# Four sequences side by side in the sample attention of a hybrid layer: one change, read from the trace

## What is computed

```python
def sample_layer(x, cache_cmp, cache_slc, cache_win, cache_mem, ...):
    ...
    o_cmp, o_slc = nsa_global(q, pos, full_c, full_s, p, rel_bias)
    o_win = win_attention(q[:, None], pos[None, :], win_kv[:, None], kpos, rel_bias)[:, 0]
    o_nsa = nsa_combine(gn, o_cmp, o_slc, o_win)
    o_mem = mem_attention(qm, cache_mem)

def masked_softmax(s, mask, axes=-1):
    ...
    m = jnp.max(s, axis=axes, keepdims=True)
    e = jnp.where(mask, jnp.exp(s - m), 0.0)
    return e / jnp.maximum(jnp.sum(e, axis=axes, keepdims=True), 1e-30)
```

## Time and profile before

| | us |
|---|---|
| median of the runs | 2143.67 |
| the profiled execution | 2147.72 |
| its span, first to last instruction | 2145.8 |
| the phase of the sample attention in it (328.26 to 526.37) | 198.11 |
| of it round 0, from the first scores of C to the last transposes | 341.7 to 433.5 |
| round 1 | 433.5 to 526.4 |

### The profile page before, as it was taken

How to read it: one execution, slowest core, us unless ns; L and a number is a source line. 1 busy time by engine, 2 the same in 40 slices (tenths; PEclk the granted TensorE clock), 3 DMA queues, 4 the chain that set the end, 5 groups by cost and what they waited for, 6 DMA issues and landing times.

```text
span 2145.8 us, 42699 instructions
## 1 busy us (share of the span) xinstructions
PE 1979.5 (92%) x17225; PEld 1038.0 (48%) x17225; DVE 516.7 (24%) x1342; ACT 407.5 (19%) x960; POOL 335.2 (16%) x359
## 2 busy tenths in 40 slices
PE   7997887788888999995999999999999999999995
PEld 3446773535447888644334444343443434444342
DVE  2224454241650111115211212112121211212111
ACT  3133561011650000000111111111111111111110
POOL 0010000000760000320112121121211112121121
PEclk9997987887999999996899999999999999999997
DMA  8116414231205110001999999999999999999994
GB/s 299 63 49 246 156 51 196 98 138 49 92 1 207 50 59 30 15 30 39 413 390 396 395 395 396 390 397 394 395 396 395 392 391 394 398 394 397 391 398 143
DMA packets 104369, 532.05 MB, mean 248 GB/s; under 512 B 15480, under 2 KB 32640, under 8 KB 52577
## 3 DMA queue, kind: packets, MB, share of 16 engines
q1 hardware_dynamic: 83721, 469.42, 55.4%
q0 software_dynamic: 19824, 59.12, 9.6%
q10 hardware_dynamic: 768, 2.75, 0.3%
HBM read 508.82 MB, written 28.91 MB: 251 GB/s over the span
## 4 chain that ended last, share of the span: by engine, by line
PE 49%; DMA 2%; ACT 1%; issue 0%; DVE 0%; POOL 0%; POOLq 0%; DVEq 0%
PE psum L2425 29%; PE psum L2438 16%; PE psum L2411 1%; PE psum L2474 1%; PE psum L2419 1%; DMA arena<-scr_h,arena 1%; PE psum L2464 1%; DMA y_sum<-arena 1%; ACT arena L2349 1%; POOL y_sum L2320 0%; ACT arena L2354 0%; DVE arena L2376 0%; PE psum L2455 0%; DVE arena L2372 0%; ACT arena L2335 0%
## 5 line engine op out<-in xcount | busy, mean ns | idle before, releaser
L2425 PE MATMUL psum<-arena 128*32 128x512 f32 x6144 | 666.9, 591 | 0.0
L2425 PEld LDWEIGHTS psum<-arena 128*32 128x32 f32 x6144 | 200.9, 108 | 447.3 <-issue 441.5
L2438 PE MATMUL psum<-arena 128*32 128x256 f32 x6144 | 344.8, 379 | 8.2 <-ACT arena L2349 8.2
L2438 PEld LDWEIGHTS psum<-arena 128*32 128x32 f32 x6144 | 191.3, 109 | 143.8 <-ACT arena L2349 15.7
L2390 DVE TENSOR_SCALAR arena<-psum 128x256 f32<-128x256 f32 x96 | 40.8, 425 | 883.0 <-PE psum L2425 880.3
L2320 POOL DMA_INDIRECT y_sum<-arena x96 | 149.3, 1555 | 620.1 <-ACT arena L2354 614.1
L2114 PE MATMUL psum<-arena 128*128 128x272 f32 x768 | 181.8, 394 | 1.4 <-PEq L217 1.4
L2114 PEld LDWEIGHTS psum<-arena 128*128 128x128 f32 x768 | 146.2, 191 | 34.8 <-issue 3.1
L2346 ACT ACTIVATE arena<-arena 128x256 f32<-128x256 f32 x96 | 40.1, 418 | 607.2 <-DVE arena L2390 607.2
L738 PE MATMUL psum<-arena 128*128 128x512 f32 (+3 forms) x320 | 112.5, 510 | 0.2 <-DVE arena L610 0.2
L2354 ACT ACTIVATE arena<-psum,arena 128x256 f32<-128x256 f32 x96 | 45.2, 471 | 187.4 <-PE psum L2438 187.4
(11 more groups left out here) (353 smaller groups left out, 1755.2 us busy)
## 6 DMA issues: line engine op xcount, KB each, us to landing
arena<-in_w_gu SPq DMA_DIRECT2D x256, 1024.0 KB, 20.1
arena<-in_w_down SPq DMA_DIRECT2D x128, 1024.0 KB, 16.9
arena<-in_w_gb SPq DMA_DIRECT2D x24, 512.0 KB, 3.5
arena<-in_w_tok SPq DMA_DIRECT2D x3, 2048.0 KB, 10.3
arena<-in_x_all SPq DMA_DIRECT2D x8, 512.0 KB, 5.9
arena<-in_cache_mem SPq DMA_DIRECT2D x8, 512.0 KB, 3.6
arena<-in_cache_win SPq DMA_DIRECT2D x8, 512.0 KB, 4.1
arena<-in_w_up SPq DMA_DIRECT2D x1, 4096.0 KB, 13.4
```

Source lines behind the costliest of these rows:

```text
L2425: mm = pe.matmul(gu_bank(g)[32 * j:32 * j + 32].rearrange("p (h n) -> p h n", h=2), xgT[:, k, 32 * g:32 * g + 32], w_in_e[:, k, :, 256 * j ...
L2438: mm = pe.matmul(dn_half(g)[32 * j:32 * j + 32], actT[:, g, k % 2, 32 * (k // 2):32 * (k // 2) + 32], w_down_e[:, k, 256 * j:256 * j + 256 ...
```

## The change

Each engine's part of the phase is written anew. A batch is now one branch (for S one chunk) of all four sequences: TensorE turns the keys of all four into four banks (`turn_keys`, 16 transposes) and then issues the four products one behind the other, each in its own 32-column part (`score`). The values follow the same way, chunk outside, sequence inside, with the 32-row product at the end. Bias and maximum are one VectorE instruction on each bank (`biased`, in the profile CUSTOM_DVE with a read of the accumulator), and the maximum over the parts is taken over a few columns. The mask of S is added to the bias on GpSimd. Both rounds of C stand at the front. The order of the other branches is M, S, W in round 0 and M, W, S in round 1. All four memory loads of round 1 wait for all window products of round 0, all four window loads of round 1 for all memory products of round 1, and the gathers of round 1 for all S products of round 0; the third and fourth of these gathers wait also for the memory loads. ScalarE copies the S bias, one bank at a time, in place of VectorE. Buffers that were shared by both rounds are doubled where both are alive.

```diff
+        BATCH = [(0, M, 0)] + [(0, S, q) for q in range(4)] + [(0, W_, 0), (1, M, 0), (1, W_, 0)] + [(1, S, q) for q in range(4)]
...
+                filled(sp, 2, "mv", 0)
+                for s in range(4):
+                    load_window(0, s)
+                filled(sp, 2, "wv", 0)
+                for s in range(4):
+                    load_memory(sp, 1, s)
+                filled(sp, 3, "mv", 1)
+                for s in range(4):
+                    load_window(1, s)
...
                 for r in range(2):
+                    if r:
+                        filled(pool, 3, "sv", 0)
                     for s in range(4):
-                        if r:
-                            pool.wait_ge(s_vu, s + 1)
                         if r and s == 2:
                             pool.wait_ge(s_ml[3], 32)
...
+                    pool.wait_ge(d_pk, r + 1)
+                    pool.tensor_tensor(blocks_of(scores[:, 0:PAST]), blocks_of(bias_slc),
+                                       pick[:, r, 3, 0:32].unsqueeze(1).unsqueeze(3).to_broadcast([128, SUB, 32, 4]),
+                                       ALU.add).then_inc(d_sb, 1)
...
+                def biased(out, scores_in, bias, r, at):
+                    return dve.tensor_tensor_reduce(out, scores_in, bias, -1.0, 3e38, ALU.add, ALU.min, stats[:, r, at:at + 1])
...
+                def quarter(n):
+                    r, _, q = BATCH[n]
+                    filled(dve, n % 2, "S", n)
+                    sl = scores[:, 512 * q:512 * q + 512]
+                    if q == 0:
+                        dve.wait_ge(d_sb, r + 1)
+                    biased(sl, bank(n % 2), sl, r, 6 + q).then_inc(free[n % 2], 1)
...
-                    link(dve.tensor_tensor(blocks_of(scores[:, 0:PAST]), blocks_of(bias_slc),
-                                           pick[:, 3, 0:32].unsqueeze(1).unsqueeze(3).to_broadcast([128, SUB, 32, 4]),
-                                           ALU.add))
-                    keys(r, S)
-
-                    for q in range(4):
-                        dve.wait_ge(s_sp, SP0 * r + 5 + 12 + q + 1)
-                        sl = scores[:, 512 * q:512 * q + 512]
-                        link(dve.tensor_tensor(sl, bank(q), sl, ALU.add))
-                    dve.wait_ge(s_sp, SP0 * r + 22)
-                    link(dve.tensor_tensor(scores[:, PAST:], bank(4)[:, 256:288], bias_new[:, r], ALU.add))
-                    maximum(k + 2, scores)
...
+                def turn_keys(n):
+                    r, kind, q = BATCH[n]
+                    for s in range(4):
...
+                        to_fill(pe, 4 + s, "K", n)
+                        for a in range(4):
...
+                            mm = pe.transpose(bank(4 + s)[:, 128 * a:128 * a + 128], src, ident)
+                        mm.then_inc(full[4 + s], 1)
...
+                        for s, rows in enumerate(rows_of_seq):
+                            mm = pe.matmul(bank(b)[rows], q_rows[:, 4 * r + s], kT(n, s), start=True, stop=True,
+                                           tile_position=(0, 32 * s))
+                    mm.then_inc(full[b], 1)
...
+                    for a in range(SUB + 1):
...
+                        for s, rows in enumerate(rows_of_seq):
+                            lhs, v = (probT[:, a, rows], cache[:, s, 256 * a + 128:256 * a + 256]) if a < SUB else \
+                                     (probT[0:32, 16, rows], v_slc[0:32, 4])
+                            mm = pe.matmul(bank(3)[rows, 0:128], lhs, v, start=(a == 0), stop=(a == SUB),
+                                           tile_position=(0, 32 * s))
```

More of the change, by code:

```diff
@@ new lines, in build_program, with to_fill, filled, emptied @@
+        use_no = {}
+        for b, name in IN_BANKS:
+            use_no[b, name] = sum(1 for b_, n_ in use_no if b_ == b)
+        bank_of = lambda *name: next(b for b, n_ in use_no if n_ == name)
+        def to_fill(pe, b, *name):
+            if use_no[b, name]:
+                pe.wait_ge(free[b], use_no[b, name])
+        def filled(eng, b, *name):
+            eng.wait_ge(full[b], use_no[b, name] + 1)
+        def emptied(eng, b, *name):
+            eng.wait_ge(free[b], use_no[b, name] + 1)
@@ new lines, in _, with exponentials, compressed @@
+                for b in range(4):
+                    filled(act, b, "bias", b)
+                    copy(bias_slc[:, 512 * b:512 * b + 512], bank(b)).then_inc(free[b], 1)
+                def exponentials(kind, r, out, in_, at_max, at_sum, scale=-1.0):
+                    return act.activation(out, in_, ACT.Exp, bias=stats[:, r, at_max:at_max + 1], scale=scale,
+                                          accum_out=stats[:, r, at_sum:at_sum + 1])
+                def compressed(r):
+                    act.wait_ge(d_mx, max_no(C, r))
+                    exponentials(C, r, p_cmp[:, r, 0:NCMP_S], p_cmp[:, r, 0:NCMP_S], 0, 1).then_inc(d_ex, 1)
@@ new lines, in _ @@
+                small(0)
+                small(1)
+                keys(0)
+                compressed(0)
+                compressed(1)
+                memory_max(0)
+                importance(0)
+                importance(1)
+                first_rows(0)
+                choose(0)
+                first_rows(1)
+                choose(1)
+                memory_turned(0)
+                keys(1)
+                memory_rows(0)
+                keys(2)
+                keys(3)
+                quarter(1)
@@ L1359, in _ @@
+                window_turned(1)
+                window_rows(1)
+                keys(8)
+                keys(9)
+                keys(10)
+                quarter(8)
+                keys(11)
+                quarter(9)
+                quarter(10)
+                quarter(11)
+                selected_max(1)
+                selected_turned(1)
+                selected_rows(1)
             @block.tensor
             def _(pe):
+                rows_of_seq = [slice(32 * s, 32 * s + 32) for s in range(4)]
```

668 lines of the change are left out of this document (369 added, 299 removed).

## The result

The kernel now takes 2075.14 us, the median of four runs (2074.06 to 2075.82), beside 2144.77 us for the kernel before on the same chip (four runs, 2143.18 to 2148.55): a ratio of 0.9672, with an interval of 0.9659 to 0.9686. The forecast was 2065.5 us, its own range 2055 to 2080. The profiled execution took 2075.44 us, with a span of 2073.6.

What follows compares the result with a forecast made beforehand. TensorE was taken to set most of the pace, the rest being waits. Followed step by step, the phase ends 78.2 us earlier: 2147.7 becomes 2069.5, less 4.05 for the median gives 2065.5 us, range 2055 to 2080.

Steps and rivals of the forecast that it cites:

- to the end of the first M: Phase start: fourth gather lands at 354.3, then four transposes (0.6) and M values (1.09); first M ends at 356.0.
- S and W scores, round 0: Round 0: first key turn at 1.2 GHz 3.7, three at 1.87, four products at 0.97; 13.2 us, then biases and maximum.
- to the end of the values, round 0: Round 0: exponential 2.25, transposes 1.9, W wait 2.7, S values 4.2 at low clock plus 1.7, W values 1.4; 14.2 us.
- memory loads, with the keys turned: New wait before M of round 1: four loads issued behind the last W product, 9.3 us, plus 0.5 for last transposes.
- window loads, with the keys turned: After M of round 1: the same wait again, 9.8 us, since the buffer is free only after the M values.
- S scores, round 1: Round 1: turns 3.7 + 3 x 1.87, three products 2.9, then copy 0.7, biases 0.8 each, maximum 0.4; given as 15.0 us.
- the four parts: Scores and values: products in four column parts run side by side, 3.96 times the rate; eight score passes 0.97 us.
- Rival parts in sequence: Scores and values: the four parts run one after the other, 65 us more at 2.4 GHz, 2131 us; chance 0.03.
- the copies set the pace: Rival, score batches: key turns wait for PSUM copies and bias, 4.3 instead of 2.84 us a batch, 2077 us; chance 0.12.
- Two gathers are under way here: 9.3, and 0.5 for the last transposes.: Round 1's memory loads: priced 9.3 us from earlier back-to-back loads beside gathers, plus 0.5 for transposes.
- and if not, 2 us are lost: Before the first M: the second C's added VectorE work just fits; if it does not, 2 us are lost.
- The clock stays low: Rival, whole phase: new waits in quick succession keep TensorE's clock low, 25 us more, 2091 us; chance 0.16.

Runs made afterwards that it cites:

- score_by_seq: Against the changed kernel, seven of twelve batches issue each score product straight behind the next sequence's turned keys, not all four together; 2096.29 us, one run.
- values_by_seq: Against the changed kernel, the S values run with the sequence outside and chunk inside, the 32-row products still last; 2094.98 us, one run.
- hold_gathers: Against the changed kernel, all four gathers of round 1, not only the last two, wait for the memory loads; 2078.3 us, ratio to before 0.9693.
- memory_in_slot_nohold: Round 1's memory loaded early into the fourth gather's buffer, mask sum late, but gathers 0 to 2 not waiting for memory loads, against the changed kernel; 2063.5 us.
- mask_late: Against the changed kernel, GpSimd's sum of mask and bias in round 0 waits until both rounds of C are through; 2074.81 us, one run.
- memory_in_slot: Against the changed kernel: round 1's memory into the fourth gather's buffer, window loads before M, gathers 0 to 2 wait for memory, mask sum late; 2058.4 us.
- max_apart: Against the changed kernel, S bias is a plain sum and one maximum over all 2,080 columns follows at the end; 2084.9 us, ratio to before 0.9707.

## Why the prediction was nearly right, and which step failed

Step by step, from the start of the phase (322.2 in this profile):

| step | forecast us | measured us |
|---|---|---|
| to the end of the first M | 27.7 | 31.1 |
| S and W scores, round 0 | 15.1 | 13.8 |
| to the end of the values, round 0 | 14.2 | 11.5 |
| memory loads, with the keys turned | 9.8 | 19.6 |
| M of round 1 | 7.0 | 7.2 |
| window loads, with the keys turned | 9.8 | 11.6 |
| W of round 1 | 9.1 | 9.4 |
| S scores, round 1 | 15.0 | 15.0 |
| the end | 12.2 | 11.2 |
| phase | 119.9 | 130.3 |

The phase is 10.4 us longer than forecast. In this profile the code ahead of it, which is unchanged, ended 6.0 us earlier than in that of before, and the code behind it took 1.5 more, so that 5.9 of the 10.4 are left in the profiled execution (2075.4 against 2069.5). The forecast was near partly by luck: these 6.0 us lie outside the phase, and inside it the two steps of round 0 that came out 4.0 us shorter than forecast hide part of the 15.0 by which the first M and the loads came out longer. The median lies 9.6 us above the forecast; the 3.7 beyond 5.9 come from the 4.05 that the forecast took off, since the profile of after lies only 0.3 above its median. The items of the S scores in round 1 add up to 15.7 and not to the 15.0 that the forecast has for them, which were measured.

*Right: the four parts.* Eight score passes take 1.00 us from start to start (forecast 0.97) and the values 4.05 (5.9 with the clock falling, 3.6 without). Against products that follow one another that is 3.9 times the rate for the scores (4 x 0.98 in score_by_seq) and 3.4 times for the values (0.101 against 0.030 us a pass), where the prediction's sum went by 3.96; values_by_seq and score_by_seq show that it is the order that gives it. Rival parts in sequence is refuted for this order. That the copies set the pace is refuted too: the period is 2.89 us, not 4.3, with no wait between batches. The fused maximum is worth what the trace of before had for the plain one, and some clock.

*Failed: "Two gathers are under way here: 9.3, and 0.5 for the last transposes."* The step took the landing of a similar load as the price, 9.3 us from the first issue to the last landing. But there the last two gathers had been issued at 436.0 and 437.3, some 10 us ahead of the loads; here they go out 2.9 and 1.7 us ahead. The runs fit a price by the bytes that stand ahead and beside. Two gathers of 2.1 MB each and four loads of 0.52 MB make 6.3 MB; busy time by stretch of the changed kernel:

```profile
381.00:395.00 14.00, 1.99 (x9) 1.35 (x10) 0.00 (x0) 1.75 (x7) 0.00 (x0) 0.55 0.98 410
```

At 410 GB/s they take 15.3 us, an estimate; TensorE's last wait for them ended 17.1 us after the first gather's issue (377.54 to 394.60), and the last load landed after 19.5. In hold_gathers four gathers and four window loads, 10.5 MB, would take 25.6 us, and the last of these loads landed 27.3 us after the first gather's issue. The step is 9.8 us longer than forecast: 1.9 for a release that came late (below), 4.8 for the loads (14.1 us from their first issue to the end of TensorE's last wait, forecast 9.3), and 3.1 for the transposes behind them, 12 at 1.2 GHz in 3.60 us, where the forecast had four in 0.5. hold_gathers shows the cause from the other side, since without gathers the same loads landed in 3.3 to 7.5 us, and memory_in_slot_nohold again. The Trainium skill (DMA: Bandwidth & Descriptors, section "Queues, rings and completion order") says that each DMA engine takes its queues by turns, a packet from one and then the next. The trace agrees in that the first memory load landed at 391.0, ahead of the second gather (393.9), which had been issued 1.7 us before it; no run here shows single packets.

*Too small: the window.* 5.24 us of wait, less than forecast, but 16 transposes at 1.2 GHz follow in three pieces (412.13 to 417.0, 4.9 us), where the forecast had 0.5.

*Too small: the first M.* "and if not, 2 us are lost": they were, 2.1 by mask_late, for a reason that the step did not name, VectorE held up by GpSimd's sum, whose cover it had only looked for on GpSimd's side. Of the 3.4 us by which the step is longer, 1.3 lie between the fourth gather's landing as forecast (26.0 us from the start) and VectorE's release (27.3); 1.3 are key transposes, eight at 1.2 GHz behind the release where the forecast had four (1.9 us, forecast 0.6), and 0.8 the M values at 1.2 GHz (1.9, forecast 1.09).

*The clock.* The low stretch came where the new waits are, 380 to 427 us, and the scores and values of round 0 ran at 1.00 outright; rival "The clock stays low" held for a third of the phase, which the forecast had mostly counted, but not for the key transposes behind the two load waits.

*Open.* After the values of round 0, VectorE's scaled sum of the W rows (L1412) and the memory loads both began 1.9 us after TensorE's last value pass. In hold_gathers and memory_in_slot, where no gather is issued just then, TensorE's wait there is 0.53 us instead of 2.33; in memory_in_slot_nohold, where three are issued, it is 3.62. In each of the seven kernels with gathers at this place, with two or with three, VectorE starts 0.7 to 0.8 us after the issue of the last one has ended (378.80 + 0.94 and 380.53 in the changed kernel). So the release follows the end of these issues; how they hold it up is not shown.

## What to carry to other kernels

Put products for different column parts of the array next to each other in TensorE's queue, with nothing between them: the same passes took a third of the time when the parts took turns as when 32 passes of one part stood in a row. Price a transfer by the bytes in flight in front of and beside it over the measured rate, not by the landing time of a like load that had other neighbours; and before holding one transfer back, ask which wait it will be in front of next. A wait on TensorE can cost more than its length: in max_apart 2.15 us more of wait brought 2.2 us more behind it, as the clock fell.

## What the runs showed of the hardware that I had not expected

A VectorE comparison of two inputs in SBUF, 33 columns wide, took 2.35 us beside a GpSimd sum and 0.19 without it; a sum of the same width with one input in PSUM took 0.18 beside it. The Trainium skill (GPSIMD Engine Reference, section "Specifications") says that GpSimd shares its interfaces to SBUF with VectorE, and names instructions with two inputs in SBUF among those that collide. The trace agrees: the comparison waited for the rest of the GpSimd instruction, 2.3 of its 3.65 us.

128 passes of 128 columns, by sequence, ran one after the other at 0.101 us each (12.95/128), although each sequence has its own column part; by chunk 136 took 0.030 each (4.05/136). In M's products four passes of a part in a row did not keep the parts apart; at which number between four and 32 the overlap ends was not measured.
